# Moving two large tensors apart in SBUF by a fixed distance, and interleaving residuals with scale rows in a decoder-layer kernel

## What is computed

```python
mod = silu(c) @ w_ada + b_ada                      # six vectors of 1024
shift1, scale1, gate1, shift2, scale2, gate2 = split(mod, 6)
h = rms_norm(x, norm1_g) * (1 + scale1) + shift1
proj = h @ w_in                                    # q, k, v, indexer, pool input, two gates
attn = indexer_selected_attention(...) @ w_attn_br
pool = multiscale_pool(...) @ w_pool_br
merged = sigmoid(g_attn) * attn + sigmoid(g_pool) * pool
x = x + gate1 * (merged @ w_out)
h2 = rms_norm(x, norm2_g) * (1 + scale2) + shift2
up = h2 @ w_up                                     # 1024 -> 2 x 2816
x = x + gate2 * ((silu(conv3(up_a)) * conv3(up_b)) @ w_down)
```

## The kernel before

| tensor | offset before | offset modulo 2048 |
|---|---|---|
| `wsplit` | 32896 | 128 |
| `hT` | 86272 | 256 |
| arena (`own[0]`, `qT`, `guT`; `merged` at +16 KB) | 119040 | 256 |

## Time and profile before

### The profile page before, as it was taken

One profiled execution on the slowest core, in us unless ns is written; L12 is line 12 of the kernel. 1 busy time (PEld: TensorE's weight loads), 2 busy tenths in 40 slices (PEclk: granted clock), 3 DMA queues, 4 the chain that ended last, 5 costly groups with the idle time before them and its releaser, 6 DMA issues.

```text
span 751.2 us, 9512 instructions
## 1 busy us (share of the span) xinstructions
PE 732.7 (98%) x3536; PEld 582.7 (78%) x3536; DVE 385.2 (51%) x706; ACT 307.6 (41%) x507; POOL 300.6 (40%) x159
## 2 busy tenths in 40 slices
PE   5899999999999999999899999999999999999997
PEld 3667688877777778888698888887888888888886
DVE  3458999944455517699855445555434432004002
ACT  6325532576567633341645343343344343121120
POOL 1001548735232335474316444344334434444340
PEclk9899999999999999999999999999999999999999
DMA  9991412211221237394095234234234133142401
GB/s 320 389 389 57 127 57 74 95 57 57 92 78 57 63 111 263 136 314 150 1 332 145 61 108 113 68 101 113 57 112 111 59 110 112 31 149 74 140 0 56
DMA packets 87307, 92.74 MB, mean 123 GB/s; under 512 B 2275, under 2 KB 69599, under 8 KB 87263
## 3 DMA queue, kind: packets, MB, share of 16 engines
q1 hardware_dynamic: 84927, 83.23, 34.3%
q10 hardware_dynamic: 2336, 8.92, 3.1%
HBM read 90.05 MB, written 2.10 MB: 123 GB/s over the span
## 4 chain that ended last, share of the span: by engine, by line
PE 95%; DVE 2%; DMA 1%; SPq 1%; ACT 1%; issue 1%; ACTq 0%; DVEq 0%
PE bank L1562 38%; PE bank L1582 24%; PE bank L1571 19%; PE bank L1632 5%; PE bank L1809 1%; PE bank L1831 1%; PE bank L1797 1%; DMA ada_first<-in_w_ada_dram 1%; PE bank L1614 1%; PE bank L1693 1%; PE bank L1866 1%; PE bank L1672 0%; PE bank L1622 0%; PE bank L1663 0%; DVE tmp_last L1453 0%
## 5 line engine op out<-in xcount | busy, mean ns | idle before, releaser
L697 POOL TENSOR_TENSOR wsplit<-stage,wsplit 128x1024 fp32r<-128x1024 f32 (+1 forms) x113 | 258.1, 2286 | 401.4 <-ACT wsplit L781 338.3
L1562 PE MATMUL bank<-hT,wsplit 128*128 128x512 f32 (+1 forms) x1120 | 263.0, 387 | 0.0
L1562 PEld LDWEIGHTS bank<-hT,wsplit 128*128 128x128 f32 x1120 | 203.7, 188 | 46.0 <-issue 1.7
L781 ACT ACTIVATE wsplit<-stage 128x1024 fp32r<-128x1024 f32 (+2 forms) x121 | 120.1, 994 | 262.5 <-PE bank L1571 174.8
L1571 PE MATMUL bank<-hT,wsplit 128*128 128x512 f32 (+1 forms) x560 | 137.3, 387 | 0.0
L1582 PE MATMUL bank<-wsplit,guT 128*128 128x512 f32 x528 | 123.4, 395 | 0.0
L1571 PEld LDWEIGHTS bank<-hT,wsplit 128*128 128x128 f32 x560 | 101.6, 188 | 22.4 <-POOL wsplit L697 0.3
L1582 PEld LDWEIGHTS bank<-wsplit,guT 128*128 128x128 f32 x528 | 99.1, 188 | 24.1
L1520 DVE SCALAR_TENSOR_TENSOR yb<-bank,conv,yb 128x511 f32<-128x511 f32 (+1 forms) x44 | 33.0, 749 | 67.4 <-ACT yb L1100 66.6
L1520 DVE SCALAR_TENSOR_TENSOR ya<-bank,conv,ya 128x511 f32<-128x511 f32 (+1 forms) x44 | 33.0, 750 | 62.4 <-ACT ya L1100 61.6
L1453 DVE TENSOR_TENSOR tmp_last<-bank,gate_row 128x512 f32<-128x512 f32 x8 | 5.5, 688 | 105.0 <-PE bank L1582 105.0
(11 more groups left out here) (193 smaller groups left out, 765.5 us busy)
## 6 DMA issues: line engine op xcount, KB each, us to landing
stage<-in_w_up_dram SPq DMA_DIRECT2D x44, 512.0 KB, 5.2
stage<-in_w_in_dram SPq DMA_DIRECT2D x14, 1024.0 KB, 5.2
stage<-in_w_down_dram SPq DMA_DIRECT2D x10, 1024.0 KB, 5.0
ada_first<-in_w_ada_dram SPq DMA_DIRECT2D x16, 512.0 KB, 8.4
ada_mid<-in_w_ada_dram ACTq DMA_DIRECT2D x8, 1024.0 KB, 6.9
ada_row<-in_w_ada_dram SPq DMA_DIRECT2D x8, 512.0 KB, 10.5
stage<-in_w_out_dram SPq DMA_DIRECT2D x4, 1024.0 KB, 6.8
ada_last<-in_w_ada_dram SPq DMA_DIRECT2D x4, 1024.0 KB, 10.3
```

Of the source, the lines that this page charges most:

```text
L697: pool.tensor_tensor(unit_split(n, 1), unit_source(n), unit_split(n, 0).bitcast(F32), ALU.subtract).then_inc(low, 1)
L781: me.did(act.activation(unit_split(n, 0), unit_source(n), ACT.Copy), high)
L1562: pe.matmul(out_bank[:, tokens], hi[:, k, :], rhs[:, part, k, tokens], start=k == 0 and part == 0, stop=False)
```

## The change

`ident` and `ones` (512 bytes each) move in front of `wsplit`; `halves` moves into the arena; `hT` is placed so that it lies 1024 bytes (half a row of 512 float32 columns) past `wsplit` modulo 2048. Added up in the same way, `wsplit` is then at 33920 (1152 modulo 2048), `hT` at 86144 (128 modulo 2048) and the arena at 118912 (128 modulo 2048). `own` and `merged` stay 0 bytes apart modulo 2048.

In the stretch between `w_out` and up, DVE makes only rows 0 to 2 of scale2 ahead of `gate_vector(0)`, and puts the other five between the residuals. ACT's `scaled(0)` waits for six rows instead of eight, and the high parts of the first up tiles come after it. On TensorE `mod_columns(4)` moves from behind tile ("wo", 1, 0) to behind `x2_turn(0)`, one tile later.

```diff
         xtok = place("xtok", [P, NT, D], F32)
+        ident = place("ident", [P, P], F32)
+        ones = place("ones", [P, P], F32)
+        split_at = at[0]
         wsplit = place("wsplit", [P, NRING, 2, WU], F32R)
         stage = place("stage", [P, NSTAGE, 2 * WU], F32)
-        ident = place("ident", [P, P], F32)
-        ones = place("ones", [P, P], F32)
-        halves = place("halves", [P, 32], F32)
...
-        at[0] += -at[0] % P
+        at[0] += (split_at + 2 * S - at[0]) % (4 * S)
         hT_at = at[0]
...
+        halves = arena("halves", [P, 32], F32, 107.0625)
...
             def scaled(t):
                 act.wait_ge(x2_inv, t + 1)
                 if t == 0:
-                    act.wait_ge(mod_sum, KD * (ROW_TURN[4] + 1))
+                    act.wait_ge(mod_sum, KD * ROW_TURN[4] + 6)
...
             for t in range(NT):
                 square_half(0, t)
-            high_parts(sch.unit["ua", 1])
             square_half(1, 0)
...
-            for k in range(5):
+            for k in range(3):
                 mod_row_of(4, k)
             gate_vector(0)
             me.settle()
-            for k in range(5, KD):
-                mod_row_of(4, k)
...
-            for t in range(NT):
-                if t == 2:
-                    mod_vector(4)
-                wo_residual(0, t)
+            wo_residual(0, 0)
+            mod_row_of(4, 3)
+            wo_residual(0, 1)
+            wo_residual(0, 2)
+            mod_row_of(4, 4)
+            wo_residual(0, 3)
...
             wo_residual(1, 0)
+            mod_row_of(4, 5)
             token_sum(0)
+            mod_row_of(4, 6)
             token_inverse(0)
+            mod_row_of(4, 7)
             for t in (1, 2):
                 wo_residual(1, t)
+                if t == 1:
+                    mod_vector(4)
+                    me.settle()
                 h2_full(t - 1, 0)
...
-                if t == 0:
+                if t == 1:
+                    x2_turn(0)
                     pe.wait_ge(gate_ok, 2)
                     mod_columns(4)
-                if t == 1:
-                    x2_turn(0)
```

More of the change, by code:

```diff
@@ L309, in build_layer @@
         base = at[0]
-        assert base + 107 * K1 + 32 <= nc.sbuf_usable_end, (base, nc.sbuf_usable_end)
+        assert base + 107 * K1 + 192 <= nc.sbuf_usable_end, (base, nc.sbuf_usable_end)
         def arena(name, shape, dt, kb):
```

## The result

The changed kernel takes 737.87 us (median of 4 runs, 736.69 to 738.09) against 755.11 us in the same comparison: ratio 0.977, 95% interval 0.976 to 0.979, so 17.2 us or 2.3% faster. Forecast were 739 us, in a range of 734 to 754. The profiled execution took 737.95 us, its span is 735.9 us against 751.2.

What follows compares the result with a forecast made beforehand. The prediction took TensorE's matmul count and spacing, plus a few short waits, to bound the kernel. Addresses 13.6 plus order 1.8 us made 15.4 off 755.1, so 739.7, stated as 739 us for a slightly quicker pace; range 734 to 754.

Steps and rivals of the forecast that it cites:

- What bounds the kernel: Whole kernel: time is a number of matmuls by what one costs, plus a few short waits; TensorE busy 732.7 of 751.2 us.
- The addresses, mechanism: Matmuls touching `wsplit`: operands 0 instead of 128 bytes apart modulo 512 take 227.3 ns, in either role; 62%.
- The rival of one role: Matmuls with `wsplit`: only one role gains, 749 us if `wsplit` moving, about 744 if the other; 8%.
- the collision: Half a row apart, the weight load may stall the moving row again: 769 us at 6 ns a matmul; 8%.
- the better distance: The new distance beats any seen: at 222 ns a matmul, 728 us or less; 6%.
- that of absolute places: Absolute place, or something else about `own`, counts: matmuls stay at 233 ns, only the order helps, 753.3 us; 16%.
- The addresses, size: 2616 matmuls of 512 columns touching `wsplit` save 14.3 us, less small losses: 13.6 us.
- The start: The 168 matmuls of line 1632 save 0.9 us at the start; half counted, so 0.5 us lost.
- The order: Between `w_out` and up: tile 2 starts at 360.6 instead of 362.36 us, 1.8 us earlier, between 0.5 and 3.2.
- the wait of near 1 us: Before `x2_turn(0)`: TensorE's wait for `xs`, 3.0 us before the change, falls to near 1 us.
- The wait for what is queued behind: At `x2_turn(1)`: DVE and ACT done near 366 against 367.4 us, cover 1.4 us; once gone, each us is lost.
- The sum: Whole kernel: 13.6 + 1.8 = 15.4 us saved, giving 738.7 from the profiled execution, 739.7 from the median, stated as 739.

Runs made afterwards that it cites:

- run 4: Kernel of float32r matmuls only, in groups of 48, sweeping the distance from weights to moving row: 226.6 ns a matmul at 1024, 229.1 at 64.
- run 1: Kernel before with only the address changes, rows and residuals in the old order: 741.67 us, ratio 0.982.
- run 5: Matmul-only kernel with four float32 matmuls ahead of each run of 8, 16 or 24: at distance 0 a run of 24 is 0.11 us shorter than at 128.
- run 7: Changed kernel with ACT's high parts of the first up tiles ahead of `square_half(1, 0)` again: 744.89 us, ratio 0.986.
- run 6: Changed kernel with `hT` and the arena 64 bytes past `wsplit` modulo 2048: 744.08 us, ratio 0.985.
- run 10: Changed kernel at distance 0, with residual ("wo", 1, 2) and all that follows it behind `h2_low(1)` on DVE and ACT: 738.75 us, ratio 0.979.
- run 8: Changed kernel with `mod_columns(4)` behind tile ("wo", 1, 0) on TensorE again: 746.00 us, ratio 0.987.

## Why the prediction was right, point by point

**What bounds the kernel.** Right. The time followed the spacing of matmuls and one wait.

**The addresses, mechanism.** Right in the step that mattered: reading `own` against `wsplit` in the earlier trace rows as a matter of distance, the same in both roles, with half a row as good as zero. The sweep shows it without the layer's other work. The period is 256 bytes, not 512; the rows of before could not tell these apart. The prediction also left out the sign: counted from the weights to the moving row, down was at 384 modulo 512 and not at 128. Only because these are the same modulo 256 did this do no harm. The rival of one role is excluded by the long stretches of the changed kernel, the collision by its result, the better distance by the sweep, and that of absolute places by run 4. The layer itself speaks against absolute places too. `own` and `merged` both lay at 0 modulo 256 before and lie at 128 now, and their matmuls kept their pace, here a timeline row of before and one of the changed kernel:

```profile
345.25 5.61 PE L1582 MATMUL bank<-own,merged 128*128 128x512 f32 x24
```

```profile
341.70 11.04 PE L1587 MATMUL bank<-own,merged 128*128 128x512 f32 x48
```

Less 0.39 us, over 23 and 47, these are 227.0 and 226.6 ns. What makes 256 bytes the period stays open: the runs show the pattern, not its cause.

**The addresses, size.** 13.6 us forecast; the addresses alone moved the span from 751.2 to 738.1, 13.1 us. Two terms were off, in opposite directions, and that the total came so close is luck. In long runs a matmul saved 6.7 ns where it had been at 233.4, not 6.0, since the 30 of 227.3 ns began right behind transposes (in run 1 the same 30 take 6.84 us, while down has its 226.7 ns). In the attention stretch, where fillers come in runs of 4 to 16 between other matmuls, I had counted the full saving and kept its loss for the range. Two lines of the chain before, then two of the changed kernel's, show what came of it:

```profile
221.52 3.73 PE bank L1562 x16
...
228.84 1.86 PE bank L1562 x8
```

```profile
220.02 3.66 PE bank L1567 x16
...
227.26 1.85 PE bank L1567 x8
```

A run of 16 saves 0.07 us, one of 8 only 0.01. By run 5, where runs of 16 and 8 save 0.07 and 0.02 us, this is the short run itself. From the 7 matmuls of line 1632 at 30 us to the start of `w_out` the changed kernel wins 3.5 us, where the prediction's 5.1 ns for each of some 1011 matmuls give 5.2. I had named other engines as the cause of a possible loss of 1.7 us there; that was the wrong cause for a loss of the right size. Up wins 5.4 us and down 3.4.

**The start.** The saving of line 1632 can't be told apart, since the first products vary by more between executions than they save (below).

**The order.** Right in sign and mechanism, too small in size. The forecast was for the start of tile 2 after `gate_sums`: 1.8 us earlier, between 0.5 and 3.2. There 3.4 us were measured (22.5 us before, 19.1 now), just past the upper bound; 2.9 us are left at the first up matmul, since 0.4 went into the new wait for `h2_low`. The term mis-sized was the start of the transposes, 16.4 us after `gate_sums` where I took 17.9: the four rows cost 1.3 us each instead of 1.6, and POOL met one residual instead of one or two rows. `xs` was therefore ready before TensorE was, and the wait of near 1 us that I had named as a sign did not come. The wait for what is queued behind I had looked for at `x2_turn(1)`; it came one step later, at `h2_low`. That the high parts cost little where they were, beyond their own 2 us, was left unsaid; run 7 shows that moving them was worth more than their length once rows lay beside them.

**The sum.** 15.4 us forecast, 15.3 us between the two spans, 17.2 us between the medians. That the first two agree so well is luck, for the spans are of single executions, and those of the kernel before went from 749.5 to 754.7 us in the later comparisons. The 1.9 us between the last two have two parts. The profiled execution of before was 1.0 us faster than its median. And the time around the span fell from 2.9 to 2.1 us: it was 1.9 to 2.1 us in every execution with the new addresses but one of run 6 (2.7), 2.6 to 3.1 in all six with the order alone, and 2.5 to 3.0 in most of before (1.9 in a few). The prediction had no such term, and the runs do not show its cause. Nor do they show why the order alone won 4.5 us between the medians and 2.9 between `gate_sums` and up. Its executions had mean granted clocks of 0.994 to 1.000, those of before 0.990 to 0.997, so part of it may be clock, lost at the start or behind the wait of 3.0 us; the one trace kept of before shows no loss behind that wait.

## What to carry to other kernels

When the same matmul line has two paces in one trace, divide the chain's stretches by their counts and compare the addresses of the operands before anything else; with float32r operands of 512 columns, place the moving tensor a multiple of 256 bytes from the weights, and test both roles, since the distance has a sign, and other widths, since 256 columns had the reverse order. It costs padding only. When work is moved off an engine's path, look at what it used to hold back: here ACT's late weight copies also kept POOL away from DVE's rows. And a longer wait of TensorE can cost more than its own length: read the granted clock of the stretch behind it.

## What the runs showed that I had not expected

- The mean spacing of float32r matmuls takes few values: 226.7 ns at multiples of 256 bytes, where it also settles to a steady one, 229.1 at 64 past them, about 233.3 at most other distances, 236.8 at 4 bytes. At 256 columns the order is reversed (5.91, 5.86 and 5.81 us for 48 at 0, 128 and 64). bfloat16 has 215.8 ns throughout.
- The launch's first products vary by up to 2.7 us with the clock granted between 20 and 30 us. The 21 matmuls at 20 us took 7.76 us in the changed kernel's profile and 5.03 us in that of run 10, with these clocks (length, PE busy and number of matmuls, clock, DMA share, GB/s), first the changed kernel, then run 10:

```profile
20.00:30.00 10.00, 9.27 (x37) 0.67 1.09 356
```

```profile
20.00:30.00 10.00, 10.00 (x56) 1.00 1.09 356
```

Two spans of single executions of one kernel can differ by more than the whole order edit is worth (733.7 to 737.2 us in run 10); leads have to be read from landmark to landmark.
- The length of a wait alone does not tell what the clock will do. Before the change TensorE idled 3.0 us ahead of `x2_turn(0)` and the granted clock stayed at 1.00. Behind 4.1 us of idling in run 7 it was 0.50. In run 8 it was 0.64 already from 350 to 351 us, though TensorE had idled only since 347.65. And ahead of the first products TensorE idles 2.0 us in both kernels shown above: the clock from 20 to 22 us was 0.50 in the changed kernel and 1.00 in run 10.
